# A two-layer hybrid decoder trunk: who turns, copies and computes the small operations of the attention loop

## The reference: what is computed

```
P = rms_norm(x) @ w_in
A: sparse attention, 4 heads: an indexer scores the keys, the top 64 per query stay (dsa_mixer)
B: a complex diagonal state-space model with 16 groups of 16 channels, then GELU and GLU (s5_mixer)
C: 8 heads, 2 kv groups: compressed, selected and window branches, summed with gates (nsa_mixer)
x = x + concat(rms_norm(A), rms_norm(B), rms_norm(C)) @ w_out
x = x + square(relu(rms_norm(x) @ w_up)) @ w_down
```

## Time and profile before

| | us |
|---|---|
| median of 3 runs | 632.72 (632.31 to 634.31) |
| the profiled execution's own time | 633.67 |
| its span in the trace | 631.9 |
| PE busy | 611.0 (97% of the span) |
| PEld busy | 504.2 (80%) |
| DVE busy | 438.8 (69%) |
| ACT busy | 358.9 (57%) |
| POOL busy | 241.5 (38%) |
| mean granted TensorE clock | 0.997 |

### The profile page before, as it was taken

One profiled execution on the slowest core, in us unless ns is written; L12 is line 12 of the kernel. 1 busy time (PEld: TensorE's weight loads), 2 busy tenths in 40 slices (PEclk: granted clock), 3 DMA queues, 4 the chain that ended last, 5 costly groups with the idle time before them and its releaser, 6 DMA issues.

```text
span 631.9 us, 10276 instructions
## 1 busy us (share of the span) xinstructions
PE 611.0 (97%) x3786; PEld 504.2 (80%) x3786; DVE 438.8 (69%) x785; ACT 358.9 (57%) x637; POOL 241.5 (38%) x422
## 2 busy tenths in 40 slices
PE   8999988999999999999999999999999999999996
PEld 7878756688888888888888787568888888888885
DVE  7699887396746667895676877748775654665664
ACT  5773789636546444444375658973654453454452
POOL 5899879505032999950004206870000000000001
PEclk9999999999999999999999999999999999999998
DMA  9675704165965665457638540325475656655631
GB/s 254 221 214 147 130 7 114 52 184 162 285 210 185 200 174 198 145 199 224 193 97 276 117 128 3 85 68 136 146 259 192 200 168 200 199 173 193 199 102 66
DMA packets 55436, 102.73 MB, mean 163 GB/s; under 512 B 12713, under 2 KB 18906, under 8 KB 55354
## 3 DMA queue, kind: packets, MB, share of 16 engines
q1 hardware_dynamic: 49130, 96.30, 50.2%
q0 software_dynamic: 1792, 4.07, 2.7%
q10 hardware_dynamic: 4464, 1.70, 1.1%
HBM read 99.69 MB, written 1.31 MB: 160 GB/s over the span
## 4 chain that ended last, share of the span: by engine, by line
PE 79%; POOL 9%; ACT 4%; issue 3%; DVE 3%; DMA 1%; SPq 1%; POOLq 0%; ACTq 0%; DVEq 0%
PE pb L1823 76%; POOL yz L622 2%; POOL sp L622 1%; ACT tab_zone L1189 1%; POOL rot L622 1%; DMA tk<-rk_hbm 1%; PE pb L1849 1%; PE pb L2250 1%; PE pb L1977 1%; SPq L455 1%; POOL sp L627 1%; ACT w_hi L943 1%; POOL dtmp L857 1%; POOL dtmp L860 1%; DVE sc_zone L1711 1%
## 5 line engine op out<-in xcount | busy, mean ns | idle before, releaser
L1386 DVE TENSOR_TENSOR w_lo<-raw,w_hi 128x1024 fp32r<-128x1024 f32 (+2 forms) x176 | 222.0, 1271 | 122.8 <-ACT w_hi L943 121.9
L943 ACT ACTIVATE w_hi<-raw 128x1024 fp32r<-128x1024 f32 (+2 forms) x184 | 188.0, 1027 | 185.8 <-PE pb L1823 174.4
L1823 PE MATMUL pb<-h_both,w_hi 128*128 128x512 f32 x512 | 181.7, 399 | 0.0
L1823 PE MATMUL pb<-h_both,w_lo 128*128 128x256 f32 x512 | 143.7, 281 | 0.0
L1823 PE MATMUL pb<-w_hi,h_both 128*128 128x512 f32 (+2 forms) x448 | 127.9, 370 | 2.4 <-DVE w_lo L1386 2.2
L1823 PEld LDWEIGHTS pb<-h_both,w_hi 128*128 128x128 f32 x512 | 96.2, 188 | 24.2 <-issue 0.6
L1823 PE MATMUL pb<-w_hi,z_hi 128*128 128x512 f32 (+1 forms) x260 | 101.0, 388 | 0.4 <-DVE w_lo L1386 0.4
L1823 PE MATMUL pb<-w_lo,z_hi 128*128 128x512 f32 (+1 forms) x260 | 100.5, 387 | 0.0
L1823 PE MATMUL pb<-w_hi,z_lo 128*128 128x512 f32 (+1 forms) x260 | 100.5, 386 | 0.0
L1823 PEld LDWEIGHTS pb<-h_both,w_lo 128*128 128x128 f32 x512 | 96.7, 189 | 0.5
L1823 PEld LDWEIGHTS pb<-w_hi,h_both 128*128 128x128 f32 x448 | 79.0, 188 | 16.8 <-DVE w_lo L1386 3.4
(11 more groups left out here) (321 smaller groups left out, 803.2 us busy)
## 6 DMA issues: line engine op xcount, KB each, us to landing
raw<-in_w_up SPq DMA_DIRECT2D x64, 512.0 KB, 4.3
raw<-in_w_down SPq DMA_DIRECT2D x64, 512.0 KB, 3.3
raw<-in_w_in SPq DMA_DIRECT2D x24, 512.0 KB, 4.5
raw<-in_w_out SPq DMA_DIRECT2D x8, 512.0 KB, 4.1
raw<-in_w_out SPq DMA_DIRECT2D x16, 256.0 KB, 4.4
raw<-in_w_in SPq DMA_DIRECT2D x8, 308.0 KB, 3.7
raw<-in_w_in SPq DMA_DIRECT2D x8, 280.0 KB, 3.3
x<-in_x ACTq DMA_DIRECT2D x4, 256.0 KB, 4.7
```

Source lines behind the costliest of these rows:

```text
L943: hi_made.by(act.activation(w_hi[:, n % RING, 0:width(n)], raw[:, n % RING, 0:width(n)], ACT.Copy))
L1386: lo_made.by(dve.tensor_tensor(w_lo[:, n % RING, 0:width(n)], raw[:, n % RING, 0:width(n)], w_hi[:, n % RING, 0:width(n)].bitcast(F32), AL ...
L1823: return pe.matmul(o, l, r, start=start, stop=stop, skip_group_check=True)
```

## The change

1. **rkv sooner** (layer 0): POOL makes `rkv` behind the doubling by 4 instead of behind that by 8.
2. **Lags sooner** (layer 0): `s5_lags` goes from behind `lo(19)` to behind the keys' roping at piece 18.
3. **Small compressed operations on POOL** (layer 0): DVE makes `x1` only; half of it and the tanh argument are made by the new `c_open2` on POOL, behind the probabilities of pair 0.
4. **`lo_out`**: in layer 0 piece 20 goes from in front of pair 0 to behind it and `c_open2`; in layer 1 piece 22 goes from behind pair 6 to behind pair 5.
5. **Compressed scores not turned** (both layers): queries stationary, keys moving, so that no copy and no transposes follow.
6. **pT shared** (both layers): for pairs 7 and 8 ACT copies bank 2 and DVE bank 3.
7. **`y_cube` behind `top`** in step 3 of layer 0, and **`u_turned` in front of `tile_out(2)`** on ACT in layer 1.

```diff
-        LO_OUT = ((None, 1, 3, 7), (None, 1, 6, 7))
+        PT_SHARED = (7, 8)
+        LO_OUT = ((0, 1, 3, 7), (None, 1, 5, 7))
...
                 for n in (1, 2, 4, 8):
                     step(double(rot, n, n))
-                if occ == 0:
-                    rstd(0, 2, rkv[:], stat[:, 2:4], A_RANK)
+                    if occ == 0 and n == 4:
+                        rstd(0, 2, rkv[:], stat[:, 2:4], A_RANK)
...
+                def c_open2():
+
+                    pool.wait_ge(c1_sb.sem, 1)
+                    ts(gt[:, 0, :], gt[:, 1, :], 0.5, None, ALU.mult)
+                    tt(gt[:, 2, :], gt[:, 1, :], gt[:, 1, :], ALU.mult)
+                    ts(gt[:, 2, :], gt[:, 2, :], 0.044715, 1.0, ALU.mult, ALU.add)
+                    tanh_in.by(pool.tensor_tensor(gt[:, 1, :], gt[:, 2, :], gt[:, 1, :], ALU.mult))
...
                     pn_sb.by(w)
+                    if L == 0 and p == 0:
+                        c_open2()
                     if p in LO_OUT[L]:
                         lo_out(20 + LO_OUT[L].index(p))
...
-                        pT_sb.by(act.activation(pT[:, 2 * (v % 2):2 * (v % 2) + 2, :], pb_all[:, 2:4, 0:384], ACT.Copy))
+                        banks = slice(2, 3 if v in PT_SHARED else 4)
+                        pT_sb.by(act.activation(pT[:, 2 * (v % 2):2 * (v % 2) + banks.stop - 2, :],
+                                                pb_all[:, banks, 0:384], ACT.Copy))
...
-                        act.wait_ge(cs_rows.sem, cs_rows.at(L, 1))
-                        cs_copy.by(act.activation(score_rows, pb[4][:, SEQ:2 * SEQ], ACT.Copy))
...
+                def pT_share(v):
+
+                    dve.wait_ge(pT_ps.sem, pT_ps.at(L, v + 1))
+                    dve.wait_ge(pv_done.sem, pv_done.at(L, v - 1))
+                    pT_half.by(dve.tensor_copy(pT[:, 2 * (v % 2) + 1, :], pb[3][:, 0:384]))
...
-                              14: (latent_heads,), 16: (queries,), 17: (far_im, far_im2, far_im3), 18: (keys_s,),
-                              19: (s5_lags, index_sum, s5_sums_read, s5_states)}
+                              14: (latent_heads,), 16: (queries,), 17: (far_im, far_im2, far_im3), 18: (keys_s, s5_lags),
+                              19: (index_sum, s5_sums_read, s5_states)}
...
+                if L == 0:
+                    between[3].remove(y_cube)
+                    between[3].append(y_cube)
+                for v in PT_SHARED:
+                    between[v + 2].append(lambda v=v: pT_share(v))
...
-                    for j in range(4):
-                        m = mm(pb[4][32 * j:32 * j + 32, SEQ:2 * SEQ], kbd[:].rearrange("p g n -> p (g n)"),
-                               cqT[:, j, :], True, True)
-                    cs_rows.by(m)
...
                     for t in range(TT):
+                        for j in range(4):
+                            m = mm(pb[4][:, t * PART + 32 * j:t * PART + 32 * j + 32], cqT[:, j, t * PART:(t + 1) * PART],
+                                   kbd[:].rearrange("p g n -> p (g n)"), (t, j) == (0, 0), True)
                     cs_ps.by(m)
...
+                        if v - 1 in PT_SHARED:
+                            pe.wait_ge(pT_half.sem, pT_half.at(L, v - PT_SHARED[0]))
...
+                        if v in PT_SHARED:
+                            pe.wait_ge(pT_half.sem, pT_half.at(L, v + 1 - PT_SHARED[0]))
```

More of the change, by code:

```diff
@@ L371, in trunk @@
         c2_sb = sig("c2_sb", 1)
[L372 removed]
+        cs_ps = sig("cs_ps", 1)
         cs_max = sig("cs_max", 1)
@@ L394, in trunk @@
         yk_sb = sig("yk_sb", 1)
+        pT_half = sig("pT_half", 2)
+        c1_sb = sig("c1_sb", 0)
         yk_half = sig("yk_half", 1)
@@ L1055, in _ @@
                                         uc.rearrange("p s (l h) -> p l s h", l=4), ACT.Copy))
-                for n in range(14, 16):
-                    hi(L, n)
-                tile_out(2)
                 def u_turned():
@@ L1064, in u_turned @@
                                            pb[0][:].rearrange("p (l q c) -> p l q c", l=4, q=4), ACT.Copy))
+                for n in range(14, 16):
+                    hi(L, n)
+                if L:
+                    u_turned()
+                tile_out(2)
                 def s5_tables():
```

19 lines of the change are left out of this document (9 added, 10 removed).

## The result

The changed kernel takes **629.86 us** (median of 22 runs, 628.48 to 635.83) against 633.74 us for the kernel before in the same comparison (22 runs): a ratio of 0.9949, 95% interval 0.9931 to 0.9967. By the ratio that is some 3.2 us (2.1 to 4.4), by the two medians 3.9 us. The forecast was 627.2 us, a gain of 5.5 us, with a range up to 629.8. The direction was right and the size was not: the measured time lies 0.06 us outside the range. The execution profiled after the change took 631.72 us with a span of 630.0.

The account below looks back on a forecast made before the run. PE was taken as the bound, busy for 97% of the span. Gains of 3.2 us in layer 0 and 2.3 us in layer 1 made 5.5 us, taken from the median 632.72 to 627.2 us; range 625.7 to 629.8.

Parts of the forecast that it names:

- pT shared (layer 0): End of layer 0's loop: halving ACT's copy releases PE's last transposes sooner, gaining 0.6 us.
- u turned sooner (layer 1): Layer 1: ACT's copy of turned u no longer follows the tile's two copies, so PE's 1.1 us wait goes.
- scores (layer 1): Layer 1: ACT's copy of the compressed scores goes, gaining 0.3 us; the added PE products are covered.
- piece 22 and pT (layer 1): Layer 1 loop: moving piece 22 and shortening ACT's copies removes PE's 0.9 us wait at pairs 8 and 9.
- Is the shift kept inside the loop: Layer 0 loop: POOL still weights pairs 1 and 2 in time; moving small operations and piece 20 costs and gains nothing.
- Rival 3: Layer 0: four small POOL operations take 5.6 instead of 1.3 us, POOL becomes the bound; 634.1 us, chance 0.06.
- Lags: Layer 0: lag transfer issued 2.4 us earlier, the 14.3 us from issue to product moves with it; gain 2.4 us.
- Rival 1: Layer 0 lag read-back: other loads on the DMA engines keep the landing at 80.7; 2.4 us lost, 629.6 us, chance 0.17.
- Compressed scores: Both layers: ACT's copy goes, gaining 0.2 us in layer 0, 0.3 in layer 1; PE's net +0.8 is covered by waits.
- Rival 2: Both layers: the new scores lie on PE's path, net 0.8 us each, 1.6 us in all; 628.8 us, chance 0.12.
- The step from the profile to the median: Whole kernel: the profiled 633.67 us stood 0.95 us above the median 632.72, so 628.2 became 627.2 us.
- signs given: Both layers: expected shorter waits, earlier near product and last transposes if right; near product at 80 us or later if wrong.

Follow-up runs that it names:

- e3: Changed kernel with layer 0's small compressed operations back on DVE and POOL's piece 20 back ahead of pair 0; ratio 0.9944 to the kernel before.
- e1: Changed kernel with the compressed scores again computed in rows, copied by ACT and turned, in both layers; ratio 0.9947 to the kernel before.
- e4: Changed kernel with ACT copying both banks of pT for pairs 7 and 8; ratio 0.9956 to the kernel before.
- e7: Changed kernel with POOL's layer 0 pieces behind pairs 1, 2, 3 and 7 instead of 0, 1, 3 and 7; ratio 0.9953 to the kernel before.
- e9: Changed kernel with SP issuing the eight lag-table reads ahead of the loads of pieces 22 and 23; ratio 0.9942 to the kernel before.
- e11: Kernel before with only the eight lag-table reads issued ahead of the loads of pieces 22 and 23; 631.78 us against 633.28, ratio 0.9967.
- e13: Changed kernel with y_cube back in its old place ahead of top in layer 0; ratio 0.9946 to the kernel before.
- e5: Kernel before, unchanged, profiled a second time; ratio 0.9998 to the kernel before.
- e10: Changed kernel with the next layer's four s_c loads issued by SP behind the lag-table reads instead of by POOL; ratio 0.9948 to the kernel before.
- e12: Changed kernel with POOL's layer 0 pieces behind pairs 1, 2, 3, 7, lag-table reads before piece 22 and 23 loads, layer 0 scores turned again; 628.86 us.
- e6: Changed kernel with POOL's last layer 0 piece, 23, behind pair 9 instead of ahead of pair 8; ratio 0.9964 to the kernel before.
- e2: Changed kernel with the lags' correction back behind piece 19 on DVE, rkv still sooner; ratio 0.9969 to the kernel before.

## Why the forecast missed

The sum, term by term, with what the runs show:

| step of the forecast | forecast | measured |
|---|---|---|
| rkv and lags sooner (layer 0) | 2.4 | 2.0 (scores 4 in e3; the near product 1.5 in the changed kernel, 2.2 in e3) |
| small operations and piece 20 (layer 0) | 0 | -0.8 (changed kernel against e3) |
| copy of the scores gone, products covered (layer 0) | 0.2 | -0.6 (e1) |
| pT shared (layer 0) | 0.6 | 0.6 (e4) |
| u turned sooner (layer 1) | 1.1 | 1.1 (scores 0 of layer 1: 24.62, now 23.48) |
| scores (layer 1) | 0.3 | 0.1 (e1) |
| piece 22 and pT (layer 1) | 0.9 | 0.7 (0.44 of it pT, e4) |

The measured 2.0, -0.8, -0.6 and 0.6 make 1.2 of the 2.26 us of layer 0. The 2.0 is taken from the first profile of the kernel before; beside the second, whose scores 4 stand at 23.48, nothing would be left of it. The -0.8, the -0.6 and the 0.6 compare variants with the changed kernel and don't depend on that. The other 1.0 us come between scores 4 and 9, where the forecast had nothing. Most of them have a place: from scores 4 to scores 5 the kernel before took 4.46 us and e1, with the same short products, 3.62. The kernel before waited there:

```profile
92.15 0.93 PE L1823 MATMUL pb<-u_zone 64*128 64x128 f32 x8 [0.78 <-DVE nmx L1711]
```

and e1 does not. Edit 7, which the forecast counted at nothing, is the likely cause, since it takes DVE's idle 0.92 us out from in front of these maxima; but no run has the short products with `y_cube` in its old place and the other edits in, and in the second profile of the kernel before the wait was 0.24 us only.

**Step "Is the shift kept inside the loop" is where it failed first: it put edits 3 and 4 at nothing, and they cost 0.8 us.** It followed POOL's times to see whether pairs 1 and 2 would be weighted in time, and they were. It did not ask what piece 20 would stand beside. In front of pair 0 it had held two of DVE's small operations already (1.63 us for two of 32 columns in the kernel before), but ahead of maxima for which DVE then still waited for PE's scores; behind pair 0 it holds the GELU ahead of the maxima of pair 3, for which PE waits. Rival 3 had the right pair of engines and the wrong direction: it priced POOL's small operations beside DVE, which cost 0.22 to 0.32, and not DVE's small operation beside POOL's large one.

**Step "Lags": the issue moved as said, the landing less.** In executions with an early start the write is issued 2.2 us sooner (2.24 behind the states in e3 and e7, for 4.42), close to the 2.4. The profiled changed kernel started late and had 1.67 of it. The trip from issue to product, which I carried over as 14.3 us, is no constant: 12.6 us in the second profile of the kernel before, 14.3 in the first, 14.5 in the changed kernel, 15.0 in e7. Rival 1 named the cause (the weights of pieces 22 and 23 and POOL's loads on the same engines), and e9 to e11 agree with it; its all-or-nothing form was wrong. And all of this was worth little, because of the pin: e9 wins the whole wait and not a hundredth of the layer.

**Step "Compressed scores": +0.2 was forecast for layer 0, -0.6 came.** The price on PE was inside the bounds (1.80 us measured, 1.3 to 2.2 bounded). The cover was what failed. The wait "right behind for the maximum" was there in the kernel before, 0.78 us at scores 5 in the row above. But in the changed kernel with short products (e1) it is gone without the help of the long ones, most likely by edit 7, and a wait that another edit takes away covers nothing. With `y_cube` in its old place (e13) the long products do fill that wait: scores 5 stand 4.84 us behind scores 4 there as in the changed kernel, against 4.46 in the kernel before. Rival 2 had the size right for layer 0 and was wrong for layer 1, where the copy's going gave 0.14 in all. By the Trainium skill, page "TensorE: Matmul & The Clock Gate", section "LDWEIGHTS (loading the stationary operand)", 16 loads of 128 columns take 1.7 us, an estimate from its rule. The 1.80 us here agree with it.

**The step from the profile to the median.** I took 0.95 us off because the profiled execution stood above a median of three runs. Over 22 runs the kernel before has 633.74 us, beside which the profiled 633.67 was an ordinary one. That is 0.95 of the 2.7 us between forecast and result, and the layers are 1.3. The remaining 0.4 are open; a late start, which the changed kernel passes on to its end and the kernel before takes up, could be the reason, but two medians of 22 runs may differ by as much. Without the 0.95 the time would have fallen inside the range, and the mechanism would have been as wrong: that the miss of the range was small says nothing for the steps.

Of the signs given: no wait for `rkv`, none for `uu`, the four POOL operations within 1.5 us and under 0.5 us left of the earlier trace rows came true. Not true: the wait of `tk` at most 0.5 us (1.5), the near product 2 to 2.5 us earlier (1.52, counted from the states), and the last transposes of layer 0 3.2 us earlier (2.28). The first sign of being wrong, a near product at 80 us or later, came true by the trace's own time (81.41), but 2.2 us of that are the late start.

## What to carry to other kernels

When a large instruction of GpSimd is moved, look at what VectorE does in the new place as well as at GpSimd's own times: a 32-column operation on the path of the next maxima took 2.00 us for 0.16 here, nearly the whole length of the large one. A wait that is removed only counts up to the next chain that does not pass through it, so before costing a gain in full, follow the other chain into the same instruction; and call an added cost covered only where a wait stands behind that very instruction and no other edit of the same change takes it away. Loads that nobody needs soon belong behind a small transfer that an engine is waiting for: moving one line for that gave about half of this change's gain. And profile the kernel before twice: its layer 0 differed by 2.8 us between two executions.

## What the runs showed of the hardware

**VectorE's small operation is held by GpSimd's large one.** An operation of two SBUF operands and 32 columns took 0.16 us alone, 1.18 us when it started 1.2 us into GpSimd's subtraction of 1024 columns, and 2.00 us when it started 0.4 us into it: in both cases it ends within 0.05 us of that instruction's end. The Trainium skill, page "SBUF — State Buffer", section "Who interferes with whom", has this: a VectorE instruction with two SBUF inputs and a GpSimd instruction that reads SBUF block one another, and whichever issued first keeps the ports until its end. The traces agree, and this rule, which the forecast did not apply in this direction, would have found the pin.

**The clock after a wait, and at the start.** Ahead of its first products with weights, PE waited 2.31 us in the execution after the change, and the granted clock between 10 and 20 us was 0.83; the kernel before had 1.37 us there and kept its clock in full. The windows' rows, after and then before:

```profile
10.00:20.00 10.00, 7.80 (x27) 6.34 (x28) 7.24 (x12) 9.88 (x19) 6.99 (x26) 0.83 1.09 300
```

```profile
10.00:20.00 10.00, 8.63 (x40) 6.96 (x39) 7.34 (x12) 8.93 (x19) 7.94 (x26) 1.00 1.11 305
```

Two products of 512 columns then take up to 1.06 us for 0.62 over some microseconds, and the states begin later: at 62.8 to 64.4 us in the six profiles where this happened (after, e1, e4, e5, e10, e12), at 61.4 to 62.3 in the ten others. The wait alone does not decide it: 1.7 us of it went with a fallen clock in e5 and with a full one in e6. In the same way the wait of 2.3 us for `tk` was followed by a granted clock of 1.00 in the kernel before and of 0.55 in e2, and the wait of 1.8 us at scores 4 by 1.00 in e9 and 0.50 in e10; layer 0 of e2 and e10 is 5.6 to 6.3 us longer than in the changed kernel. So a wait of two microseconds on TensorE here is a risk beside its own length; what decides it is not settled by these runs.
